# Turning the recurrent outputs of 14 tiles with VectorE and block copies instead of TensorE

## The chip, the core and the metric

The kernel runs on one core of a Trainium2 chip. The metric is the device time of one execution in microseconds; a profiled execution also gives a span, from its first to its last instruction. Engines are TensorE (PE; PEld is its weight load), VectorE (DVE), ScalarE (ACT), GpSimd (POOL) and SyncE (SP), which issues most DMAs. All arithmetic is float32 or the fp32r form of it.

## The reference

One inference step of a one-layer decoder trunk: a prompt of 2048 tokens, and 8 samples of 8 tokens. A norm and one input projection feed three groups of heads: a matrix-memory recurrence (mLSTM, 4 heads of 256), a short gated convolution, and cross-attention into 256 memory tokens. Their outputs go through one output projection, a residual add and a final norm. The change lies in the recurrence:

```python
num = (w_inter[..., None] * jnp.einsum('bthd,bhde->bhte', qb, C)
       + jnp.einsum('bhts,bshe->bhte', S, vb))
den = w_inter * jnp.einsum('bthd,bhd->bht', qb, n) + jnp.sum(S, axis=-1)
h = num / jnp.maximum(jnp.abs(den), jnp.exp(-m_t))[..., None]
C_new = w_C[..., None, None] * C + jnp.einsum('bhs,bshd,bshe->bhde', w_s, kb, vb)
...
h = jax.nn.sigmoid(heads(o_pre)) * h
h = rms_norm(h, g_head.reshape(ML_HEADS, ML_HEAD_DIM))
y_ml = h.reshape(B, T, ML_WIDTH) * jax.nn.silu(z_ml)
...
y = jnp.concatenate([y_ml, y_cv, y_xa], axis=-1) @ w_out
```

## The kernel before

The program runs in stages: the input projection with its splits (to about 1400 us), the convolution and cross-attention with their part of the output projection, and the recurrence with the rest of the output projection, from about 1605 us to the end. The change touches the last stage, the function `recur`.

There the prompt goes by in 16 tiles of 128 tokens (`NT`). Between them run 8 units for the samples: a unit has its front part in an even tile (`front_of`) and its back part in the odd tile behind (`back_of`). Each engine has one instruction stream, written out by hand in the loops over `t`; semaphores in `S` tie them together. In one tile:

- TensorE: `numerators(t)` (four heads, L2249 from the state C, L2250 from the score weights), in odd tiles the unit's numerators (L2376, L2379), then eight `update(t, j)` (L2264), one for each half head of the state, with the products of the output projection of tile t-1 between them (`out_part`, L2294 to L2296; in even tiles two parts behind each update, in odd tiles one, and eight behind the last). In odd tiles a ninth small update (L2267) and the unit's own update (L2277) follow the eighth. Then `scores(t + 1)` (L2225), the unit's front (L2360, L2362) or the turn of its output (L2387), and `turn_y(t)` (L2342): eight 128x128 transposes of the tile's output y from `th[t % 2]` into banks 3 and 4.
- The updates alternate between two banks, `DC = (0, 5)`. Update j may start when VectorE has added update j-2 to the state: `wait(pe, S["C_updated"], updates_before(t) + j - 1)`. The scores use bank 0 and wait for all updates.
- VectorE: `add(t - 2)` (L2626), `first_half(t)` (L2700 to L2709: the numerators times the output gate, the denominator), the updates of the state (L2725) with turns between them: `turn_v` (L2673), behind update 5 `final_norm(t - 2)` (L2648), behind update 6 `turn_keys(t + 1)` (L2682, from the staging tile `kb` into `kw`). Then `second_half(t)` (L2732, L2737: y times coef), in odd tiles the unit's update (L2749) and second half (L2780, L2783), `turn_o(t + 1)` (L2692), `score_weights(t + 1)` (L2618), `y_gate(t)` (L2656: y from banks 3 and 4 times z) and `y_low(t)` (L2663).
- `numerators(t)` has at its head `pe.wait_ge(S["sw_ready"], t + 1)`, the score weights of L2618.
- ScalarE: exponentials of the weights (L2450), squares for the norms (L2474, L2480), the gate's tanh (L2487), the unit's values (L2496, L2497), `keys(t + 1)` (L2458), the unit's front (L2521, L2523), `y_high(t)` (L2509).
- GpSimd: mask add (L2143) and query products (L2147) for the next tile, and small powers (L2165, L2169) for the norms, each between the squares of ScalarE and the scaling by VectorE.
- SyncE issues loads in a fixed order: in `key_squares(t)` the keys of a later tile, in 128x1024 values, into `kb`, as soon as the last ones have been turned; behind them the output gates and z.

VectorE's transpose turns each 32x32 block in its place, so a tile loaded "in squares" (`load_squares`) comes out turned as a whole.

Of the kernel before, what the change touches and what calls it, by code (L numbers as in the profile page):

```python
# [19 lines left out]
ALU = mybir.AluOpType  # L20
# [10 lines left out]
NT = T // P  # L31
# [12 lines left out]
KM = 8  # L44

SQ = 32
# [1865 lines left out]
def recur(nc, block, before, S, overlay, bank, w, ident, raw, last_y, work, wide, syhl, area, nT, mask, smask, columns, late_w, res, yh, yl,  # L1912
# [39 lines left out]
    late_h, late_l = late_w  # L1952
    LAST_X = 2 * TILES

    OUT, SPARE, DC = (6, 7), 5, (0, 5)
    SOUT, FOLD = (1, 2), (3, 4)

    def unit(u):
        return u // 4, u % 4

    def split_y(t):
# [59 lines left out]
    def _(sp):  # L2021
# [22 lines left out]
        def key_squares(t):  # L2044
            if SQUARES_FROM <= t < NT:
                wait(sp, S["keys_turned"], t - SQUARES_FROM)
                load_squares(sp, w, 2, kb[:, :], t, S["kb_loaded"])

# [83 lines left out]
    def _(pool):  # L2132
# [55 lines left out]
        pool.wait_ge(S["set"], 3)  # L2188
        for t in range(NT):
            ahead(t + 1)  # L2190
            power("squares_ready", 4 * t + 4, ssq[:, :], msq[:, :], rinv[:, :], 0.25 / HD, "rinv_ready")
            if back_of(t) is not None:
                power("s_squared", back_of(t) + 1, sssq[:, :], smsq[:, :], srinv[:, :], 0.25 / HD, "s_rinv_ready")
            if front_of(t) is not None:
                ahead_unit(front_of(t))
            if t >= 2:
                out_norm(t - 2)
        out_norm(NT - 2)
        half_norm(NT, "s_out_squared", "s_out_begun", "s_out_mean", "s_out_rstd")
# [3 lines left out]
    def _(pe):  # L2203
# [25 lines left out]
        def numerators(t):  # L2229
# [9 lines left out]
            for h in range(H):  # L2239
                if h < 2:  # L2240
                    if t < SQUARES_FROM:
                        pe.wait_ge(S["kw_ready"], 4 * t + 2 * h + 2)
                else:
                    wait(pe, S["y_gated"], 2 * (t - 1) + h - 1)
                num = bank[1 + h][:, 0:HE]
# [148 lines left out]
        for t in range(NT):  # L2394
# [34 lines left out]
            if front_of(t) is not None:  # L2429
                unit_front(t, front_of(t))  # L2430
            if t < NT - 1:
                turn_y(t)
# [11 lines left out]
    def _(act):  # L2444
# [54 lines left out]
        def y_high(t):  # L2499
# [7 lines left out]
            for i in range(2):  # L2507
                act.wait_ge(S["y_gated"], 2 * t + i + 1)
                act.activation(split_y(t)[0][:, 4 * i:4 * i + 4, :], z[:, 4 * i:4 * i + 4, :], ACT.Copy).then_inc(S["y_high"], 1)  # L2509

        def store(s):
            act.wait_ge(S["out_ready"], s + 1)
            act.dma_start(tile_rows(y_prompt[0], s), acc[s % ACC][:, :]).then_inc(S[f"y_stored{s % ACC}"], 16)
# [23 lines left out]
        for t in range(NT):  # L2537
# [12 lines left out]
            if front_of(t) is not None:  # L2550
                unit_vo_back(front_of(t))
            keys(t + 1)
            if front_of(t) is not None:
                unit_front(front_of(t))
# [31 lines left out]
    def _(dve):  # L2586
# [64 lines left out]
        def y_gate(t):  # L2651
            dve.wait_ge(S["z_loaded"], 16 * (t + 1))
            for i in range(2):
                zi = z[:, 4 * i:4 * i + 4, :]
                dve.wait_ge(S["y_turned"], 2 * t + i + 1)
                dve.tensor_tensor(zi, bank[3 + i].ap().rearrange("p (f t) -> p f t", f=4), zi,  # L2656
                                  ALU.mult).then_inc(S["y_gated"], 1)
# [26 lines left out]
        def turn_o(t):  # L2684
# [5 lines left out]
            wait(dve, S["s_squared"], units_before(t))  # L2690
            wait(dve, S["y_turned"], 2 * (t - 1))
            dve.transpose(th[t % 2], vo[:, 1, :]).then_inc(S["o_turned"], 1)  # L2692
# [34 lines left out]
        def second_half(t):  # L2727
# [7 lines left out]
            for h in range(H):  # L2735
                y = th[p][:, h * HD:(h + 1) * HD]
                dve.tensor_scalar(y, y, coef[:, h:h + 1], None, ALU.mult).then_inc(S["y_ready"], 1)  # L2737

        def n_of(u):
# [58 lines left out]
        for t in range(NT):  # L2798
# [6 lines left out]
            for j in range(8):  # L2805
                update(t, j)
                if j in (1, 3):
                    turn_v(t + 1, j // 2)
                if j == 6:
                    turn_keys(t + 1)  # L2810
                if j == 5 and t >= 2:
                    final_norm(t - 2)
                if j in (4, 5) and t == 0:
                    last_add(j - 4)
            second_half(t)
            if t == NT - 1:
# [62 lines left out]
```

## Time and profile before

| | |
|---|---|
| time, median of 3 runs | 2020.84 us (2015.42 to 2021.22) |
| profiled execution | 2021.7 us, span 2019.8 us |
| granted TensorE clock, mean | 0.999 of full speed |
| TensorE busy | 2008.2 us, 99% |
| VectorE busy | 1474.5 us, 73% |
| ScalarE busy | 912.9 us, 45% |
| GpSimd busy | 874.6 us, 43% |

Busy time of TensorE counts matmuls whose ends are modelled, and they overlap: what an instruction costs is read from the distance of the starts. The times in a timeline are microseconds from the start of the span. "issue" as releaser means a wait whose releaser the profile doesn't show.

### The profile page before, as it was taken

Reading aid. Unit: us, or ns where it says so; the run is one execution under the profiler, and the core shown is the slowest. Engines: PE = TensorE matmul, PEld = TensorE weight load, DVE = VectorE, ACT = ScalarE, POOL = GpSimd, SP = SyncE. Lnnn points to the kernel's source line nnn. Section 1 sums busy time; section 2 is a strip of 40 time slices with the busy share of each in tenths; the row PEclk is TensorE's granted clock in tenths of the full one; section 3 lists DMA queues with packets and bytes.
Section 4 is the critical chain, followed back from the end, with each engine's and each line's share of the span. In section 5 each row is a group of like instructions: output and inputs, shape, how many; then the busy total and the mean of one; then the engine's idle time right before and its main releaser. Section 6 shows DMA issues by size and latency. Waiting matters only on the chain.

```text
span 2019.8 us, 34158 instructions
## 1 busy us (share of the span) xinstructions
PE 2008.2 (99%) x12151; PEld 1877.8 (93%) x12151; DVE 1474.5 (73%) x2336; ACT 912.9 (45%) x1863; POOL 874.6 (43%) x721
## 2 busy tenths in 40 slices
PE   9999999999999999999999999999999999999998
PEld 6999999999999999999999999998888888888886
DVE  7777787798778877897778767654445468777775
ACT  5554445445444455454454455442324333433332
POOL 2556555585555565575555555520000122222220
PEclk9999999999999999999999999999999999999999
DMA  6655667555646676555445566578746788888765
GB/s 205 155 142 142 150 152 162 128 141 124 152 122 152 158 171 134 137 143 122 120 131 138 126 157 144 134 212 188 172 115 183 201 250 261 272 239 237 235 180 121
DMA packets 600151, 333.69 MB, mean 165 GB/s; under 512 B 331296, under 2 KB 563888, under 8 KB 599984
## 3 DMA queue, kind: packets, MB, share of 16 engines
q1 hardware_dynamic: 561824, 312.90, 59.5%
q10 hardware_dynamic: 37008, 14.43, 2.9%
q0 software_dynamic: 1152, 4.19, 0.6%
q8 instruction: 98, 1.61, 0.4%
q14 instruction: 69, 0.57, 0.1%
HBM read 237.87 MB, written 93.58 MB: 164 GB/s over the span
## 4 chain that ended last, share of the span: by engine, by line
PE 93%; DVE 2%; SPq 2%; DMA 1%; issue 1%; ACT 0%; POOL 0%; DVEq 0%; POOLq 0%; ACTq 0%
PE bank L742 21%; PE bank L744 21%; PE bank L743 21%; PE bank L2294 3%; PE bank L2296 2%; PE bank L2295 2%; PE bank L2264 2%; PE bank L2249 2%; PE bank L1650 1%; PE bank L1651 1%; PE bank L1652 1%; PE bank L1636 1%; PE bank L1639 1%; PE bank L1637 1%; PE bank L1601 1%; PE bank L1566 1%
## 5 line engine op out<-in xcount | busy, mean ns | idle before, releaser
L742 PE MATMUL bank<-xh,wh 128*128 128x352 f32 x2688 | 869.3, 323 | 0.9 <-DVE stage L1111 0.9
L744 PE MATMUL bank<-xh,wl 128*128 128x352 f32 x2688 | 867.0, 323 | 0.0
L743 PE MATMUL bank<-xl,wh 128*128 128x352 f32 x2688 | 863.6, 321 | 0.0
L1093 DVE TENSOR_TENSOR wl<-raw,wh 128x512 fp32r<-128x512 f32 x384 | 407.4, 1063 | 166.5 <-ACT wh L881 165.5
L742 PEld LDWEIGHTS bank<-xh,wh 128*128 128x128 f32 x2688 | 504.6, 188 | 3.8 <-issue 2.0
L743 PEld LDWEIGHTS bank<-xl,wh 128*128 128x128 f32 x2688 | 507.4, 189 | 0.3 <-issue 0.2
L744 PEld LDWEIGHTS bank<-xh,wl 128*128 128x128 f32 x2688 | 506.3, 188 | 0.0
L903 ACT ACTIVATE snap<-bank 128x352 f32<-128x352 f32 x384 | 178.5, 465 | 374.3 <-PE bank L744 374.2
L881 ACT ACTIVATE wh<-raw 128x512 fp32r<-128x512 f32 x384 | 240.6, 628 | 156.8 <-PE bank L744 155.6
L1093 DVE TENSOR_TENSOR wl<-wt,wh 128x512 fp32r<-128x512 f32 x288 | 246.8, 860 | 85.1 <-ACT wh L881 84.2
L692 POOL TENSOR_TENSOR stage<-snap 128x352 f32<-128x352 f32 x96 | 100.8, 1050 | 440.7 <-ACT snap L903 428.1
L881 ACT ACTIVATE wh<-wt 128x512 fp32r<-128x512 f32 x288 | 180.2, 626 | 118.9 <-PE bank L744 112.7
L676 POOL TENSOR_TENSOR wt<-raw 128x512 f32<-128x512 f32 x96 | 153.6, 1600 | 56.0 <-DMA raw<-in_w_in 42.1
L683 POOL TENSOR_TENSOR wt<-raw,wt 128x512 f32<-128x512 f32 x96 | 154.8, 1613 | 49.8 <-DVE wl L1093 49.8
L1111 DVE TENSOR_TENSOR stage<-bank,snap 128x352 f32<-128x352 f32 x288 | 149.0, 517 | 34.8 <-PE bank L744 30.6
L2143 POOL TENSOR_TENSOR work<-area,mask 128x512 f32<-128x512 f32 x16 | 20.7, 1295 | 336.8 <-DMA area<-scr_a 211.2
L679 POOL TENSOR_TENSOR wt<-raw,wt 128x512 f32<-128x512 f32 x96 | 156.0, 1625 | 8.1 <-DVE wl L1093 0.7
L680 POOL TENSOR_TENSOR raw<-raw 128x512 f32<-128x512 f32 x96 | 158.7, 1653 | 0.0
L2294 PE MATMUL bank<-wm_h,out_yh 128*128 128x512 f32 x240 | 117.1, 488 | 0.0
L2296 PE MATMUL bank<-wm_h,out_yl 128*128 128x512 f32 x240 | 94.3, 393 | 0.0
L2295 PE MATMUL bank<-wm_l,out_yh 128*128 128x512 f32 x240 | 94.0, 392 | 0.0
L2725 DVE SCALAR_TENSOR_TENSOR m_wide<-m_wide,wcb,bank 128x257 f32<-128x257 f32 x120 | 56.9, 475 | 49.6 <-PE bank L2264 48.4
(346 smaller groups left out, 2599.0 us busy)
## 6 DMA issues: line engine op xcount, KB each, us to landing
raw<-in_w_in SPq DMA_DIRECT2D x72, 1024.0 KB, 5.8
raw<-in_w_in SPq DMA_DIRECT2D x48, 512.0 KB, 5.6
scr_vob<-stage SPq DMA_DIRECT2D x192, 88.0 KB, 3.6
scr_qk<-stage SPq DMA_DIRECT2D x48, 352.0 KB, 5.2
raw<-scr_qk SPq DMA_DIRECT2D x16, 1024.0 KB, 8.8
area<-scr_vob SPq DMA_DIRECT2D x32, 512.0 KB, 8.0
scr_acc<-x_res SPq DMA_DIRECT2D x17, 512.0 KB, 6.2
m_acc<-scr_acc SPq DMA_DIRECT2D x17, 512.0 KB, 7.6
```

Source lines behind the costliest of these rows:

```text
L676: pool.tensor_tensor(wt[:, 0], b12, b11, ALU.subtract).then_inc(S["t_ready"], 1)
L679: pool.tensor_tensor(wt[:, 1], b22, wt[:, 0], ALU.subtract).then_inc(S["t_ready"], 1)
L680: pool.tensor_tensor(b12, b22, b12, ALU.subtract).then_inc(S["t_ready"], 1)
L683: pool.tensor_tensor(wt[:, 2], b21, wt[:, 1], ALU.subtract).then_inc(S["t_ready"], 1)
L742: pe.matmul(out, wh[:, b, k, :], xh[:, b, k, :], start=(first and k == 0), stop=False, skip_group_check=True)
L743: pe.matmul(out, wh[:, b, k, :], xl[:, b, k, :], start=False, stop=False, skip_group_check=True)
L744: m = pe.matmul(out, wl[:, b, k, :], xh[:, b, k, :], start=False, stop=(k == 3), skip_group_check=True)
L881: act.activation(halves(q, b)[0], source(q, b), ACT.Copy).then_inc(S["w_high"], 1)
L903: act.activation(snap[:, n, :], g if n == 1 else b, ACT.Copy).then_inc(S["snap"], 1)
L1093: dve.tensor_tensor(low, source(q, b), high.bitcast(F32), ALU.subtract).then_inc(S["w_low"], 1)
L1111: dve.tensor_tensor(out, src, snap[:, add, :], ALU.add).then_inc(S["out_dve"], 1)
L2294: pe.matmul(out, h[:, k, :], wmh[:, k, c], start=(k == 0), stop=False)
```

## The change

The outputs of tiles 1 to 14 (`IN_BLOCKS`) are no longer transposed by TensorE. VectorE turns `th[t % 2]` (128x1024) in 32x32 blocks into the staging tile `kb` with one instruction. The 16 blocks of partitions and columns are then carried back into `th[t % 2]` at their place, in copies of 32 partitions by 8x32 values: 8 by ScalarE, 8 by GpSimd. `y_gate` then reads `th` in SBUF instead of the banks. As the source of the turn must be ready earlier, in these tiles the key turn and the second half stand behind update 5, the turn of y behind update 6 and the final norm behind update 7. The load of the next keys into `kb` waits for both sets of copies. Tiles 0 and 15 stay as they were.

```diff
+    ysq = kb[:, :].rearrange("p (k f t) -> p k f t", f=4, t=SQ)
+    IN_BLOCKS = range(1, NT - 1)
+    BLOCKS = [(a, f) for a in range(4) for f in range(4)]
+    ACT_MOVES, POOL_MOVES = BLOCKS[:8], BLOCKS[8:]
...
+    def y_moved(t, a, f):
+        return th[t % 2].rearrange("p (k x) -> p k x", k=KM)[SQ * f:SQ * (f + 1), :, SQ * a:SQ * (a + 1)]
...
         def key_squares(t):
             if SQUARES_FROM <= t < NT:
                 wait(sp, S["keys_turned"], t - SQUARES_FROM)
+                wait(sp, S["y_moved"], len(ACT_MOVES) * (t - SQUARES_FROM))
+                wait(sp, S["y_carried"], len(POOL_MOVES) * (t - SQUARES_FROM))
                 load_squares(sp, w, 2, kb[:, :], t, S["kb_loaded"])
...
+            if t - 1 in IN_BLOCKS:
+                pool.wait_ge(S["y_carried"], len(POOL_MOVES) * (t - 1))
             ahead(t + 1)
...
             if t >= 2:
                 out_norm(t - 2)
+            if t in IN_BLOCKS:
+                pool.wait_ge(S["y_squared"], t)
+                pool.wait_ge(*((S["out_rstd"], t - 1) if t >= 2 else (S["s_rinv_ready"], back_of(t) + 1)))
+                for a, f in POOL_MOVES:
+                    pool.tensor_copy(y_moved(t, a, f), ysq[SQ * a:SQ * (a + 1), :, f, :]).then_inc(S["y_carried"], 1)
...
-                else:
-                    wait(pe, S["y_gated"], 2 * (t - 1) + h - 1)
+                elif t == 1:
+                    pe.wait_ge(S["y_gated"], h - 1)
+                elif h == 2:
+                    wait(pe, S["s_vo_ready"], sum(front_of(x) is not None for x in range(t)))
...
-            if t < NT - 1:
+            if t < NT - 1 and t not in IN_BLOCKS:
                 turn_y(t)
...
+        def y_moves(t):
+            act.wait_ge(S["y_squared"], t)
+            for a, f in ACT_MOVES:
+                act.activation(y_moved(t, a, f), ysq[SQ * a:SQ * (a + 1), :, f, :], ACT.Copy).then_inc(S["y_moved"], 1)
...
         def y_gate(t):
             dve.wait_ge(S["z_loaded"], 16 * (t + 1))
+            if t in IN_BLOCKS:
+                dve.wait_ge(S["y_moved"], len(ACT_MOVES) * t)
+                dve.wait_ge(S["y_carried"], len(POOL_MOVES) * t)
+                for i in range(2):
+                    zi, c = z[:, 4 * i:4 * i + 4, :], slice(512 * i, 512 * (i + 1))
+                    dve.tensor_tensor(zi, th[t % 2][:, c].rearrange("p (f t) -> p f t", f=4), zi,
+                                      ALU.mult).then_inc(S["y_gated"], 1)
+                return
...
+        def turn_y(t):
+            dve.wait_ge(S["y_ready"], 4 * t + 4)
+            dve.transpose(kb[:, :], th[t % 2]).then_inc(S["y_squared"], 1)
...
                 if j in (1, 3):
                     turn_v(t + 1, j // 2)
+                if t in IN_BLOCKS:
+                    if j == 5:
+                        turn_keys(t + 1)
+                        second_half(t)
+                    if j == 6:
+                        turn_y(t)
+                    if j == 7 and t >= 2:
+                        final_norm(t - 2)
+                    continue
```

TensorE at the end of an odd tile, before (`raw` holds queries and keys, `m_s_o` the unit's output, `m_wide` here y and then the scaled queries):

```order
L2296 MATMUL bank<-wm_h,out_yl 128x512
L2225 MATMUL bank<-raw 128x128 x8
L2387 MATMUL bank<-ident,m_s_o 128x128 x2
L2342 MATMUL bank<-ident,m_wide 128x128 x8
L2249 MATMUL bank<-m_wide 128x257 x2
L2250 MATMUL bank<-area,work 128x257
```

and now, with the line numbers of the changed kernel:

```order
L2317 MATMUL bank<-wm_h,out_yl 128x512
L2244 MATMUL bank<-raw 128x128 x8
L2408 MATMUL bank<-ident,m_s_o 128x128 x2
L2270 MATMUL bank<-m_wide 128x257 x2
L2271 MATMUL bank<-area,work 128x257
```

The eight transposes between the scores and the numerators are gone; nothing took their place.

VectorE in an odd tile from update 4 on, before (`m_kb` is the staging tile `kb`, the unnamed 128x257 products are the updates):

```order
L2673 STREAM_TRANSPOSE area<-area 128x2x256
L2725 SCALAR_TENSOR_TENSOR m_wide<-m_wide,wcb,bank 128x257 x2
L2648 SCALAR_TENSOR_TENSOR m_acc<-m_acc,m_few,m_gf 128x1024
L2725 SCALAR_TENSOR_TENSOR m_wide<-m_wide,wcb,bank 128x257
L2682 STREAM_TRANSPOSE m_wide<-m_kb 128x1024
L2725 SCALAR_TENSOR_TENSOR m_wide<-m_wide,wcb,bank 128x257
L2732 SCALAR_TENSOR_TENSOR m_few<-m_few 128x4
L2737 TENSOR_SCALAR m_wide<-m_wide,m_few 128x256 x4
L2716 TENSOR_TENSOR m_s_C<-m_s_C,m_wide 128x8
```

and now:

```order
L2709 STREAM_TRANSPOSE area<-area 128x2x256
L2761 SCALAR_TENSOR_TENSOR m_wide<-m_wide,wcb,bank 128x257 x2
L2718 STREAM_TRANSPOSE m_wide<-m_kb 128x1024
L2768 SCALAR_TENSOR_TENSOR m_few<-m_few 128x4
L2773 TENSOR_SCALAR m_wide<-m_wide,m_few 128x256 x4
L2761 SCALAR_TENSOR_TENSOR m_wide<-m_wide,wcb,bank 128x257
L2777 STREAM_TRANSPOSE m_kb<-m_wide 128x1024
L2761 SCALAR_TENSOR_TENSOR m_wide<-m_wide,wcb,bank 128x257
L2676 SCALAR_TENSOR_TENSOR m_acc<-m_acc,m_few,m_gf 128x1024
L2752 TENSOR_TENSOR m_s_C<-m_s_C,m_wide 128x8
```

Key turn and second half moved ahead of update 6, the turn of y was added ahead of update 7, and the final norm went behind it. The even tiles have the same order without the last row.

## Rows read from the trace of the kernel before

**Rows 1.** The chain of waits of the whole page, by engine (share of the span).

```profile
PE 93%; DVE 2%; SPq 2%; DMA 1%; issue 1%; ACT 0%; POOL 0%; DVEq 0%; POOLq 0%; ACTq 0%
```

**Rows 2.** Line L2342, output transposes: ns min/median/max, first and last start, forms.

```profile
L2342 PE MATMUL bank<-ident,area x64: 272/273/307, 1620.8 to 1968.0; 128*128 128x128 f32 x64
```

**Rows 3.** Timeline, end of an even tile (start us, length us, engine, line; idle before, releaser).

```profile
1720.64 0.69 DVE L2618 SCALAR_TENSOR_TENSOR work<-bank,work 128x512 f32<-128x512 f32 x1 [0.34 <-issue]
1720.85 0.94 PEld L2342 LDWEIGHTS bank<-ident,area 128*128 128x128 f32 x8
1721.76 0.74 PEld L2249 LDWEIGHTS bank<-m_wide 128*128 128x128 f32 x4
```

**Rows 4.** Timeline, end of an odd tile.

```profile
1746.86 0.69 DVE L2618 SCALAR_TENSOR_TENSOR work<-bank,work 128x512 f32<-128x512 f32 x1 [2.52 <-issue]
1747.62 0.73 PEld L2249 LDWEIGHTS bank<-m_wide 128*128 128x128 f32 x4
```

**Rows 5.** Timeline, tile 0 to 1, where TensorE waits for the score weights.

```profile
1621.25 0.65 DVE L2618 SCALAR_TENSOR_TENSOR work<-bank,work 128x512 f32<-128x512 f32 x1
1621.98 0.73 PEld L2249 LDWEIGHTS bank<-m_wide 128*128 128x128 f32 x4 [0.30 <-issue]
```

**Rows 6.** Timeline, updates 5 to 8 of an odd tile.

```profile
1734.98 0.48 DVE L2725 SCALAR_TENSOR_TENSOR m_wide<-m_wide,wcb,bank 128x257 f32<-128x257 f32 x1 [0.65 <-PE bank L2264]
1736.96 1.24 DVE L2682 STREAM_TRANSPOSE m_wide<-m_kb 128x1024 f32<-128x1024 f32 x1
...
1737.51 0.64 PEld L2267 LDWEIGHTS bank<-m_few,work 128*128 128x128 f32 x4
1738.12 0.44 DVE L2725 SCALAR_TENSOR_TENSOR m_wide<-m_wide,wcb,bank 128x257 f32<-128x257 f32 x1
1738.49 0.15 DVE L2732 SCALAR_TENSOR_TENSOR m_few<-m_few 128x4 f32<-128x4 f32 x1
1739.73 0.17 DVE L2716 TENSOR_TENSOR m_wide<-m_wide 128x8 f32<-128x8 f32 x1
```

**Rows 7.** Timeline, updates 5 to 7 of an even tile and the scores behind them.

```profile
1762.59 0.48 DVE L2725 SCALAR_TENSOR_TENSOR m_wide<-m_wide,wcb,bank 128x257 f32<-128x257 f32 x1 [1.32 <-PE bank L2264]
1766.66 0.48 DVE L2725 SCALAR_TENSOR_TENSOR m_wide<-m_wide,wcb,bank 128x257 f32<-128x257 f32 x1 [0.63 <-PE bank L2264]
1767.85 1.95 PE L2225 MATMUL bank<-raw 128*128 128x128 f32 x16
1769.89 0.69 DVE L2618 SCALAR_TENSOR_TENSOR work<-bank,work 128x512 f32<-128x512 f32 x1 [0.34 <-issue]
```

**Rows 8.** Timeline, tile 2.

```profile
1665.96 1.29 DVE L2648 SCALAR_TENSOR_TENSOR m_acc<-m_acc,m_few,m_gf 128x1024 f32<-128x1024 f32 x1 [2.65 <-POOL m_few L2169]
1669.22 2.05 PE L2225 MATMUL bank<-raw 128*128 128x128 f32 x16 [0.96 <-DVE m_wide L2725]
```

**Rows 9.** Timeline, VectorE's low halves: with GpSimd idle, and beside GpSimd.

```profile
1624.21 1.29 DVE L2663 TENSOR_TENSOR out_yl<-area,out_yh 128x512 fp32r<-128x512 f32 x2 [0.16 <-ACT out_yh L2509]
...
1723.21 1.82 DVE L2663 TENSOR_TENSOR out_yl<-area,out_yh 128x512 fp32r<-128x512 f32 x2 [0.16 <-ACT out_yh L2509]
```

**Rows 10.** Timeline, GpSimd's products of queries.

```profile
1609.69 2.79 POOL L2147 TENSOR_TENSOR m_wide<-raw,area 128x256 f32<-128x256 f32 x4
...
1723.42 1.07 POOL L2147 TENSOR_TENSOR m_wide<-raw,area 128x256 f32<-128x256 f32 x1 [0.65 <-PE bank L2250]
```

**Rows 11.** GpSimd's smallest one-input instruction, by form: busy us, mean ns | idle before.

```profile
L2165 POOL TENSOR_SCALAR m_few<-m_few 128x4 f32<-128x4 f32 x16 | 3.1, 193 | 66.1 <-ACT area L2474 41.8 <-ACT m_wide L2474 24.2
```

**Rows 12.** Timeline, ScalarE: four key copies of 128x256 in a row.

```profile
1766.07 1.71 ACT L2458 ACTIVATE m_kw<-m_kw,wsc 128x256 f32<-128x256 f32 x4 [0.58 <-DVE m_kw L2682]
```

**Rows 13.** Timeline, start of an odd tile: update 0 on VectorE, update 2 on TensorE.

```profile
1729.59 0.47 DVE L2725 SCALAR_TENSOR_TENSOR m_wide<-m_wide,wcb,bank 128x257 f32<-128x257 f32 x1
1730.95 0.60 PE L2264 MATMUL bank<-area,m_kw 128*128 128x257 f32 x2
```

**Rows 14.** The key staging tile: its loads, issue to landing.

```profile
DMA to landing us min/median/max: 3.6/8.4/10.6
```

More of the change, by code:

```diff
@@ L1959, in unit, with turned_by_pe @@
         return u // 4, u % 4
+    def y_moved(t, a, f):
+        return th[t % 2].rearrange("p (k x) -> p k x", k=KM)[SQ * f:SQ * (f + 1), :, SQ * a:SQ * (a + 1)]
+    def turned_by_pe(t):
+        return 2 * sum(x not in IN_BLOCKS for x in range(t))
     def split_y(t):
@@ L2552, in _ @@
             keys(t + 1)
+            if t in IN_BLOCKS:
+                y_moves(t)
             if front_of(t) is not None:
@@ L2652, in y_gate @@
             dve.wait_ge(S["z_loaded"], 16 * (t + 1))
+            if t in IN_BLOCKS:
[6 more added lines that the diff above has]
+                return
             for i in range(2):
                 zi = z[:, 4 * i:4 * i + 4, :]
-                dve.wait_ge(S["y_turned"], 2 * t + i + 1)
+                dve.wait_ge(S["y_turned"], turned_by_pe(t) + i + 1)
                 dve.tensor_tensor(zi, bank[3 + i].ap().rearrange("p (f t) -> p f t", f=4), zi,
@@ L2690, in turn_o @@
             wait(dve, S["s_squared"], units_before(t))
-            wait(dve, S["y_turned"], 2 * (t - 1))
+            wait(dve, S["y_gated"], 2 * (t - 1))
             dve.transpose(th[t % 2], vo[:, 1, :]).then_inc(S["o_turned"], 1)
@@ L2808, in _ @@
                     turn_v(t + 1, j // 2)
+                if t in IN_BLOCKS:
+                    if j == 5:
[6 more added lines that the diff above has]
+                    continue
                 if j == 6:
@@ L2814, in _ @@
                     last_add(j - 4)
-            second_half(t)
+            if t not in IN_BLOCKS:
+                second_half(t)
             if t == NT - 1:
```

## The prediction

> **What bounds the kernel now.** I read the chain of waits first: TensorE holds 93% of it [rows 1]. An edit therefore counts only through what it does to TensorE's row of work. The change touches the recurrent stage alone, about 1610 to 2019 us, so I read the timeline there: all engines around the end of an even and of an odd tile [rows 3, 4], then VectorE's updates [rows 6, 7]. The reader should look for one thing: who arrives last at each point where TensorE needs another engine. In the steady pairs of tiles TensorE never waits. The pattern repeats every 49.25 us (score weights at 1720.64 and 1769.89 [rows 3, 7]), so one pair stands for all.
>
> **What is removed.** Eight transposes a tile in 14 tiles, 112 in all. The page gives each 272 ns [rows 2], but they overlap: from the first weight load of the eight to the next instruction's load it is 1720.85 to 1721.76, 0.91 us [rows 3]. That is 14 x 0.91 = 12.7 us of TensorE, and a reader who stops here forecasts 2009.
>
> But these transposes stand in a particular gap. TensorE computes the scores of tile t+1, VectorE turns them into score weights (L2618, 0.69 us), and the numerators of t+1 wait for these weights at their head. The transposes are what TensorE did meanwhile. Tile 0 to 1 shows the wait when it decides: L2618 ends at 1621.90 and the numerators' first weight load starts at 1621.98, after 0.30 us of idleness [rows 5]; so release costs 0.08 us.
> - End of an odd tile: L2618 runs 1746.86 to 1747.55, so the numerators could start at 1747.63. They start at 1747.62 now [rows 4]. The gain is nothing: the removed 0.91 us turns into a wait of the same length. Seven tiles, 0.
> - End of an even tile: there the unit's front matmuls stand in the gap too. L2618 ends at 1721.33, release at 1721.41, and the load starts at 1721.76 now [rows 3]. At most 0.35 us a tile, 2.4 us in seven.
>
> **What is moved on VectorE.** In the 14 tiles the key turn and the second half (scaling by coef) come between updates 5 and 6, the new turn of y between 6 and 7, and the final norm behind 7. Updates used to reach TensorE promptly, and TensorE needs them: update 8 of an odd tile reuses the bank of update 6 and waits until VectorE has consumed it.
> - Odd tile: update 5 starts at 1734.98, released by TensorE. Start to start, an update takes 0.40, the key turn 1.16 (1736.96 to 1738.12), the second half 1.24 (1738.49 to 1739.73) [rows 6]. So update 6 starts at 1734.98 + 0.40 + 1.16 + 1.24 = 1737.78, ends 0.47 later at 1738.25, and is seen at 1738.33. TensorE wants to load for L2267 at 1737.51 [rows 6]. The stall is 0.82 by the loads; as a load begins while the matmul in front still runs, I take 0.7 (ends 0.6 and 0.85). Nothing gives it back: all behind it, up to the scores and L2618, hangs on TensorE. 7 x 0.7 = +4.9 us.
> - Even tile: there is no update 8. Update 5 starts at 1762.59; update 6 at +2.80 = 1765.39; the turn of y at 1765.79; update 7 at 1766.95, ends 1767.43, against 1766.66 now. The scores wait for it and start at 1767.85 [rows 7]; that holds, by little. Then final norm (1.2) and gate turn (1.2) end at 1769.8, just before L2618 at 1769.89 [rows 7]. So the 0.35 of the even tile survives if nothing lengthens this chain.
>
> **What lengthens it.** GpSimd's eight copies run just beside the final norm, which reads two operands in SBUF. The nearest pair of rows: the low halves (two SBUF operands) take 1.29 us with GpSimd idle and 1.82 beside its products [rows 9]; GpSimd's product takes 0.70 alone (2.79 for four) and 1.07 beside them [rows 10]. So the final norm may cost up to 0.5 us more, and L2618 then starts at 1770.3: the even gain is anything from 0.35 down to -0.1. I take 0.2, 7 x 0.2 = -1.4 us. The gate multiply, which read PSUM and now reads two SBUF operands beside GpSimd's mask add, can lose another 0.5. The Trainium skill ("SBUF — State Buffer", who interferes with whom) says that a VectorE instruction with two SBUF inputs contends with a GpSimd instruction that reads SBUF, and this trace agrees: 1.82 against 1.29.
>
> **The copies.** ScalarE's eight, by its four key copies of 256 columns in 1.71 us [rows 12], are 8 x 0.40 = 3.3 us (ends: 0.3 to 0.5 each, for 32 partitions with strided blocks). They start when y is turned, 1767.1 in an even tile, and the unit's key scaling behind them moves to about 1770.5, 0.2 late. GpSimd's copy is not in the trace. Below it lies its smallest one-input instruction, 0.19 [rows 11]; above it the two-input product of as many columns, 0.70 alone, 1.07 contended [rows 10]. With one operand instead of two I halve what grows: 0.19 + 0.25 = 0.45, eight in 3.6 us, about 4 with contention. "GPSIMD Engine Reference" in the Trainium skill (elementwise cycle accounting) has about one cycle per element for one input and 2.6 for two; by it the copy would be near 0.4 us and the sum would not change; no row here has such a copy.
>
> When are they needed? In an odd tile y is turned at 1739.4 and gated only after L2618, 1747.6: over 8 us, ample. In an even tile y is turned at 1767.1 and the gate comes right behind L2618 and two small instructions, 1771.1: 4 us. The gate, the low halves, the add and the first half all stand ahead of the next tile's update 0, which ends at 1730.06, while TensorE's update 2, which needs its bank, starts at 1730.95, its load some 0.2 before [rows 13]. That leaves 0.6 us, or 0.25 where TensorE has become 0.35 earlier. With 4 us for the copies and up to 0.5 on the gate, I charge 0.2 in each of six or seven odd tiles: +1.2 us.
>
> **Loads.** The next keys are now loaded into the staging tile only after the copies: in an even tile about 1771.2, in an odd one 1743.5. They land 8.4 us later, 10.6 at most [rows 14], by 1782 and 1754; they are wanted by 1784.6 (49.25 behind 1735.4) and 1763. Hidden; if the cover went, each us late is a us on updates 6. The output gates' load queued behind it slips 2 us into ScalarE slack.
>
> **Tile 2** has a hiccup: VectorE waits 2.65 us for a norm ahead of update 6, and TensorE's scores wait 0.96 for update 7 [rows 8]. The new order puts that norm behind update 7, so these 0.96 us go: -1.0.
>
> **Sum.** +4.9 - 1.4 + 1.2 - 1.0 = +3.7 us. The profiled execution took 2021.7 us (span 2019.8), so it would be 2025.4; the median before is 0.9 lower, hence 2024.5.
>
> **Rivals.**
> - A, the removed work comes back as time: 12.7 us less, near 2009. For it: TensorE is 93% of the chain. Against it: rows 4. It would need TensorE's numerators to be released by something other than L2618, or VectorE's updates not to be awaited at update 8. The milder form (no stall at update 8, even gain 0.35 whole, tile 2) is -3.4, about 2017.4. This is the other side; it decides if update 6 ends before 1737.4 in an odd tile.
> - B, the GpSimd copies end last. If one costs 0.70, eight take 5.6, 1.2 us beyond the room of about 4.4, in seven tiles +8.4; at 1.07, 8.6 us, 4.2 late, +29. With the stall at update 8 that is 2033 to 2053. For it: SBUF contention in rows 9 and 10; against it: one input only.
> - C, the contention is worse than its rows (final norm and turn both held, updates of even tiles later than 1767.5, so that the scores wait as well): another 0.3 to 0.5 in each of 14 tiles, 2029 to 2032.
>
> **Chances.** Forecast 0.55 (its own range 2021 to 2028); A 0.18, of it two thirds the mild form; B 0.15; C 0.12. About 0.3%, 6.1 us, is what can be told from no change: the borders are 2014.8 and 2026.9. Faster is strong A: 0.06. Slower is B, C and the upper fifth of the forecast: 0.37. The rest, 0.57, is no change. The range for 8 in 10 reaches from the mild A to the lower end of B: 2017 to 2036.
>
> **What would show it.** Right: L2342's successor shows only 16 transposes of y; a wait on L2618 at the head of the numerators, 0.8 to 0.9 us in odd tiles and 0.3 to 0.5 in even ones; a wait of TensorE for update 6 at update 8, near 0.7, seven times. The even gate multiply is released by L2618's chain, not by GpSimd. Wrong: no wait at update 8 (then A), a GpSimd copy over 0.55 us (then B), scores waiting for update 7 in even tiles (then C), key turns waiting for their load.

## The result: 0.8% slower, and the profile after

| | before | changed |
|---|---|---|
| time, median of 6 runs each | 2021.03 us (2015.42 to 2024.06) | 2037.64 us (2035.27 to 2041.93) |
| profiled execution, span | 2019.8 us | 2034.1 us |
| TensorE busy | 2008.2 us | 2002.9 us |
| GpSimd busy | 874.6 us | 943.6 us |

The ratio is 1.0082, 95% interval 1.007 to 1.0094. The forecast was 2024.5 us with a range to 2036: the sign of its sum was right, its size wrong by 13 us, and the measured time lies outside the range.

The page of the changed kernel, busy times and the chain of waits by engine:

```profile
PE 2002.9 (98%) x12039; PEld 1865.4 (92%) x12039; DVE 1507.0 (74%) x2350; ACT 959.4 (47%) x1975; POOL 943.6 (46%) x833
...
PE 90%; DVE 6%; issue 1%; POOL 1%; SPq 0%; ACT 0%; DMA 0%; DVEq 0%; POOLq 0%; ACTq 0%
```

The chain has moved from TensorE to VectorE, 2% before [rows 1] and 6% now. So TensorE waits. Where, the view of the waits of TensorE in the recurrent stage tells (engine, tile, line, what it waited for: us in total, times, longest):

```profile
PE bank L2285 <- DVE m_s_o L2806: 10.7, 6, 1.9
PE bank L2270 <- issue: 6.9, 14, 0.7
PE bank L2288 <- DVE m_wide L2761: 2.7, 7, 0.4
```

The second and the third were forecast: the head of the numerators and update 8. The first, the largest, was not. It is at update 1 of the odd tiles. The timeline of the changed kernel from the end of an even tile (12, score weights at 1721.69) to update 1 of the next, odd one; it answers to [rows 3, 13]:

```profile
1718.86 4.48 POOL L2216 COPY area<-m_kb 32x256 f32<-32x256 f32 x8 [6.48 <-DVE m_kb L2777]
...
1719.09 1.27 DVE L2676 SCALAR_TENSOR_TENSOR m_acc<-m_acc,m_few,m_gf 128x1024 f32<-128x1024 f32 x1
...
1721.69 0.69 DVE L2646 SCALAR_TENSOR_TENSOR work<-bank,work 128x512 f32<-128x512 f32 x1 [0.18 <-issue]
...
1722.45 0.73 PEld L2270 LDWEIGHTS bank<-m_wide 128*128 128x128 f32 x4 [0.39 <-issue]
...
1723.06 0.19 DVE L2799 SCALAR_TENSOR_TENSOR m_wide<-bank,m_wide 128x32 f32<-128x32 f32 x1 [0.60 <-ACT work L2549]
...
1723.42 1.27 POOL L2155 TENSOR_TENSOR work<-area,mask 128x512 f32<-128x512 f32 x1
...
1723.47 2.90 DVE L2686 TENSOR_TENSOR area<-area 128x512 f32<-128x512 f32 x2 [0.22 <-POOL area L2216]
...
1724.65 4.59 POOL L2159 TENSOR_TENSOR m_wide<-raw,area 128x256 f32<-128x256 f32 x4
...
1726.29 2.35 DVE L2699 TENSOR_TENSOR out_yl<-area,out_yh 128x512 fp32r<-128x512 f32 x2
...
1728.56 1.27 DVE L2654 TENSOR_TENSOR m_acc<-m_acc,bank 128x512 f32<-128x512 f32 x2
...
1729.28 0.70 PE L2285 MATMUL bank<-area,m_kw 128*128 128x257 f32 x2
...
1731.87 0.41 DVE L2806 SCALAR_TENSOR_TENSOR m_s_o<-m_s_o,bank 128x256 f32<-128x256 f32 x1
...
1732.53 0.67 PE L2285 MATMUL bank<-area,m_kw 128*128 128x257 f32 x2 [1.87 <-DVE m_s_o L2806]
```

Three things are to be seen. The numerators start 0.76 behind the start of the score weights, as predicted. The gate multiply (L2686) starts 1.78 behind them and its pair takes 2.90, the low halves (L2699) 2.35. And TensorE, after update 0 at 1729.28, sits until VectorE has finished L2806 for update 1. The same place of the kernel before, in its timeline:

```profile
1721.78 1.28 DVE L2656 TENSOR_TENSOR area<-bank,area 128x512 f32<-128x512 f32 x2
...
1724.96 1.27 DVE L2626 TENSOR_TENSOR m_acc<-m_acc,bank 128x512 f32<-128x512 f32 x2
...
1728.59 0.70 PE L2264 MATMUL bank<-area,m_kw 128*128 128x257 f32 x2
...
1728.80 0.41 DVE L2766 SCALAR_TENSOR_TENSOR m_s_o<-m_s_o,bank 128x256 f32<-128x256 f32 x1
...
1729.58 0.42 PEld L2264 LDWEIGHTS bank<-area,m_kw 128*128 128x128 f32 x2
...
1729.81 0.60 PE L2264 MATMUL bank<-area,m_kw 128*128 128x257 f32 x2
```

There the gate's pair took 1.28, and L2766 (L2806 now) ended at 1729.21. Update 1 started its matmuls 0.60 behind that end, at 1729.81. In the changed kernel, where it waits for this end (1732.28), it starts 0.25 behind it, at 1732.53. So the room was 0.35 us.

The end of the odd tile, from update 6 to the next numerators, answers to [rows 4, 6]:

```profile
1740.55 0.48 DVE L2761 SCALAR_TENSOR_TENSOR m_wide<-m_wide,wcb,bank 128x257 f32<-128x257 f32 x1
...
1741.08 0.61 PE L2288 MATMUL bank<-m_few,work 128*128 128x4 f32 x4 [0.39 <-DVE m_wide L2761]
...
1742.24 4.49 POOL L2216 COPY m_wide<-m_kb 32x256 f32<-32x256 f32 x8 [4.38 <-DVE m_kb L2777]
1742.46 1.27 DVE L2676 SCALAR_TENSOR_TENSOR m_acc<-m_acc,m_few,m_gf 128x1024 f32<-128x1024 f32 x1
...
1750.31 0.69 DVE L2646 SCALAR_TENSOR_TENSOR work<-bank,work 128x512 f32<-128x512 f32 x1 [1.85 <-issue]
...
1751.11 1.11 PE L2270 MATMUL bank<-m_wide 128*128 128x257 f32 x4 [0.68 <-issue]
1751.12 2.36 DVE L2686 TENSOR_TENSOR area<-m_wide,area 128x512 f32<-128x512 f32 x2
1751.18 1.75 POOL L2155 TENSOR_TENSOR work<-area,mask 128x512 f32<-128x512 f32 x1 [4.45 <-DVE work L2646]
```

Update 8 (L2288) waits for update 6, and the removed transposes have become a wait of 0.68 at the numerators.

**Where the time went.** I measured TensorE from start to start in every tile. One steady pair took 49.25 us and takes 51.66:

| TensorE, start to start, us | before | changed | difference |
|---|---|---|---|
| even tile, scores to numerators | 3.28 | 2.84 | -0.44 |
| odd tile, numerators to update 0 | 6.72 | 6.80 | +0.08 |
| odd tile, update 0 to 1 | 1.22 | 3.25 | +2.03 |
| odd tile, update 1 to 2 | 1.14 | 1.20 | +0.06 |
| odd tile, update 7 to 8 and what restarts behind it | 1.13 | 1.67 + 0.1 | +0.66 |
| odd tile, scores to numerators, and on to update 0 | 2.87 + 5.25 | 2.84 + 5.28 | 0 |

From tile 0's scores to tile 15's, 15.0 us were added: tiles 5, 7, 9 and 11 2.4 each, tile 13 4.0, tile 3 1.75, tiles 0 and 1 0.8 together, tile 2 gave back 1.15 [rows 8]; the span grew by 14.3.

**Tile 15 shows what the wait at update 1 needs.** It is the last tile, and at the end of tile 14 GpSimd has no mask add and no products left to do. The gate starts as late there as elsewhere, 1.78 behind the score weights (1981.61):

```profile
1983.39 1.29 DVE L2686 TENSOR_TENSOR area<-area 128x512 f32<-128x512 f32 x2 [0.22 <-POOL area L2216]
...
1984.84 1.29 DVE L2699 TENSOR_TENSOR out_yl<-area,out_yh 128x512 fp32r<-128x512 f32 x2 [0.16 <-ACT out_yh L2530]
...
1990.42 0.60 PE L2285 MATMUL bank<-area,m_kw 128*128 128x257 f32 x2
```

Both pairs take 1.29, L2806 ends 8.21 behind the score weights instead of 10.59, and update 1 follows update 0 by 1.22 without a wait. So the late start of the gate and its new source cost no time by themselves. The wait comes only with GpSimd's mask add and products beside VectorE's pairs.

Tile 13 is longer than its neighbours by 1.6, and its waits don't tell why. The windows of TensorE do (window, its length, busy us and instructions, granted clock, DMA share, GB/s):

```profile
1936.00:1940.00 4.00, 2.15 (x9) 1.00 0.92 241
1940.00:1944.00 4.00, 4.00 (x12) 0.57 0.41 34
1941.00:1942.00 1.00, 1.00 (x4) 0.50 0.49 29
```

TensorE was busy 2.15 of 4 us while it waited for update 1, and then the granted clock was 0.57 in the mean of 4 us and 0.50 inside them, 1.2 GHz instead of 2.4. A wait here can cost more than its length. That the wait brought the clock down is read from their order in time; no run shows it by itself.

### The profile page after: what moved, and what is told of

Read it like the earlier page. It is cut to its first block, busy times and chain, and to the rows that moved or that the text cites. A ratio compares the mean times of both kernels' runs of the same rounds, so it can differ in the third digit from the quotient of the medians.

```text
span 2034.1 us, 34185 instructions
## 1 busy us (share of the span) xinstructions
PE 2002.9 (98%) x12039; PEld 1865.4 (92%) x12039; DVE 1507.0 (74%) x2350; ACT 959.4 (47%) x1975; POOL 943.6 (46%) x833
## 4 chain that ended last, share of the span: by engine, by line
PE 90%; DVE 6%; issue 1%; POOL 1%; SPq 0%; ACT 0%; DMA 0%; DVEq 0%; POOLq 0%; ACTq 0%
PE bank L742 21%; PE bank L744 21%; PE bank L743 21%; PE bank L2315 2%; PE bank L2317 2%; PE bank L2316 2%; PE bank L2285 2%; PE bank L2270 2%; PE bank L1650 1%; PE bank L1651 1%; PE bank L1652 1%; PE bank L1636 1%; PE bank L1637 1%; PE bank L1639 1%; PE bank L1601 1%
```

## The experiments

The times of all are set against the kernel before on the same chip. "Gap" is TensorE's distance from update 0 to update 1 in a steady odd tile: 1.22 before, 3.25 after the change. The executions of the kernel before spread from 2015.4 to 2024.1, so a mechanism is read from the profiled executions, and the medians say only whether the time moved.

**e1, VectorE's order alone**, on the kernel before; the transposes stay on TensorE.

```diff
                 if j in (1, 3):
                     turn_v(t + 1, j // 2)
+                if 1 <= t < NT - 1:
+                    if j == 5:
+                        turn_keys(t + 1)
+                        second_half(t)
+                    if j == 7 and t >= 2:
+                        final_norm(t - 2)
+                    continue
```

> Only VectorE's new order, on the kernel before: TensorE still transposes y, no copies, gate reads PSUM. Theory (three waits of TensorE: update 8 about 0.67 us, head of the next numerators 0.9 us in odd tiles, start of the odd tiles 2.1 us, the last from contention with GpSimd at the gate): only the wait at update 8 is here, 7 x 0.67 = +4.7 us, less about 1.0 us of tile 2, so +3.7 us against before (2021), and no wait of TensorE at update 1. Rival (the order alone makes VectorE late everywhere): a wait at update 1 here too, +10 us or more.

Measured 2025.97 us (2024.54 to 2028.94), ratio 1.0039 (1.0025 to 1.0053); the medians are 7.0 us apart and the profiled spans 4.3, where 3.7 was expected. TensorE's waits in its trace:

```profile
PE bank L2267 <- DVE m_wide L2725: 2.7, 7, 0.4
```

The distance to update 8 is 1.67 in seven odd tiles, update 1 waits nowhere, and tile 2 lost its hiccup (24.19 to 23.04). Tile 1 alone became 1.1 us longer. The term for update 8 stands as predicted, and it is due to the order, not to the copies.

**e2, the gate reads SBUF**, on the kernel before. TensorE still transposes y, but in tiles 1 to 14 the gate leaves the result aside and multiplies the y that isn't turned. A wait that keeps this y until the gate has read it is not shown in the cut.

```diff
+                dve.wait_ge(S["y_ready"], 4 * t + 4)
+                src = th[t % 2][:, 512 * i:512 * (i + 1)] if 1 <= t < NT - 1 else bank[3 + i].ap()
-                dve.tensor_tensor(zi, bank[3 + i].ap().rearrange(...), zi, ALU.mult)
+                dve.tensor_tensor(zi, src.rearrange(...), zi, ALU.mult)
```

> Only the gate's source, on the kernel before: in tiles 1 to 14 the gate multiply reads y in SBUF instead of the banks. It leaves out the full transpose of y (what it reads is not turned); TensorE still does its transposes. Theory (the gate with two SBUF operands is held up beside GpSimd's mask add and query products): the gate's pair takes 2.4 to 2.9 us instead of 1.28, the low halves no less than 1.8, and TensorE waits 1.0 to 1.5 us at update 1 of the seven odd tiles: +7 to +11 us. Rival (the copies end late, the source costs nothing): pair at 1.3 us, no wait, same time as before.

Measured 2022.21 us (2017.44 to 2023.53), ratio 1.0011 (1.0 to 1.0021). From its timeline at the same place:

```profile
1720.73 2.14 DVE L2658 TENSOR_TENSOR area<-area 128x512 f32<-128x512 f32 x2
...
1722.37 1.10 POOL L2147 TENSOR_TENSOR m_wide<-raw,area 128x256 f32<-128x256 f32 x1 [0.65 <-PE bank L2250]
...
1723.03 2.12 DVE L2665 TENSOR_TENSOR out_yl<-area,out_yh 128x512 fp32r<-128x512 f32 x2 [0.16 <-ACT out_yh L2509]
```

A miss. The mechanism shows (gate pair 2.14 against 1.28, low halves 2.12 against 1.82, gap 1.50), and the 0.63 by which VectorE's chain grew less the room of 0.35 is the growth of the gap. But at 0.35 us for each odd tile it is a sixth of the effect. GpSimd's products still wait for TensorE between each other here, and VectorE gets through in their pauses; the mask add is 0.28 ahead of the gate. In the changed kernel it starts with the gate, and the products run back to back.

**e3, GpSimd's mask add and products behind the gate**, on the changed kernel.

```diff
                 pool.wait_ge(S["y_carried"], len(POOL_MOVES) * (t - 1))
+                pool.wait_ge(S["y_gated"], 2 * t)
```

> The changed kernel, with GpSimd's mask add and query products held until the gate multiply is done. Theory (contention at the gate): the gate's pair falls to about 1.3 us, the wait at update 1 of odd tiles from 2.0 to about 0.6, seven times, so 8 to 10 us less than the changed kernel, about 2028. Rival (the late copies decide): at most 1 us less. Rival (waits of ScalarE for the masks come in its place): no gain, ScalarE waiting for GpSimd before its squares.

Measured 2029.45 us (2026.92 to 2031.58), ratio 1.0053 (1.0036 to 1.007). Its timeline:

```profile
1721.18 1.29 DVE L2687 TENSOR_TENSOR area<-area 128x512 f32<-128x512 f32 x2 [0.22 <-POOL area L2217]
...
1722.61 1.27 POOL L2155 TENSOR_TENSOR work<-area,mask 128x512 f32<-128x512 f32 x1 [1.56 <-issue]
1722.63 2.93 DVE L2700 TENSOR_TENSOR out_yl<-area,out_yh 128x512 fp32r<-128x512 f32 x2 [0.15 <-ACT out_yh L2531]
```

The gate's pair is back at 1.29 us, and the low halves pay instead: 2.93. The contention moved on by one pair of instructions, and the gap fell only to 2.49, a wait of up to 1.2 us where 0.6 was expected.

**e4, update 6 ahead of the second half in odd tiles**, on the changed kernel.

```diff
                     if j == 5:
                         turn_keys(t + 1)
+                    if j == 5 + t % 2:
                         second_half(t)
```

> The changed kernel, with update 6 ahead of the second half in odd tiles (key turn, update 6, second half, turn of y). Theory: the wait at update 8 (L2288 of the changed kernel, 0.67 us in seven tiles) goes and nothing takes its place, -4.7 us against the changed kernel, about 2033. Rival (update 6 was not what it waited for): no change.

Measured 2030.92 us (2029.54 to 2034.05), ratio 1.0061 (1.0041 to 1.0081). The distance to update 8 is 1.13 again, and the gap at update 1 stays, 3.27. The two waits are independent, and the second half can be moved at no cost.

**e5, no GpSimd copies**, on the changed kernel. Eight of the sixteen blocks of y are not carried back, and the gate reads the y that isn't turned in their place. The three waits for these copies are gone as well; the cut leaves them out.

```diff
-                for a, f in POOL_MOVES:
-                    pool.tensor_copy(y_moved(t, a, f), ysq[SQ * a:SQ * (a + 1), :, f, :]).then_inc(S["y_carried"], 1)
```

> The changed kernel without GpSimd's eight copies (half of y's blocks stay where they were and the gate reads them so: the output of the prompt is wrong in them). Rival B of the prediction (the copies on GpSimd end last): the gate starts up to 1.5 us earlier and most of the 2.0 us wait at update 1 goes. Theory (the start of an odd tile is lost in three parts: gate released 0.64 late, gate 1.4 longer, low halves 0.5 longer): ScalarE's copies still hold the gate back, and mask add and query products fall apart again, so the gate's pair takes about 2.1 as where only its source was changed; gap between updates 0 and 1 from 3.25 to about 2.2 us, 7 to 8 us less in all.

Measured 2027.35 us (2026.49 to 2032.14), ratio 1.0037 (1.0024 to 1.005). At the same place of its trace, an even tile's end:

```profile
1726.25 0.69 DVE L2641 SCALAR_TENSOR_TENSOR work<-bank,work 128x512 f32<-128x512 f32 x1 [0.18 <-issue]
...
1727.11 1.27 POOL L2154 TENSOR_TENSOR work<-area,mask 128x512 f32<-128x512 f32 x1 [10.16 <-DVE work L2641]
...
1727.74 2.33 DVE L2680 TENSOR_TENSOR area<-area 128x512 f32<-128x512 f32 x2
...
1728.67 0.85 POOL L2158 TENSOR_TENSOR m_wide<-raw,area 128x256 f32<-128x256 f32 x1 [0.28 <-PE bank L2266]
...
1729.99 1.86 DVE L2693 TENSOR_TENSOR out_yl<-area,out_yh 128x512 fp32r<-128x512 f32 x2
```

GpSimd's mask add starts 0.86 behind the score weights instead of 1.73, its products are spread out again (1728.67 and on), the gate starts at +1.49 instead of +1.78, and the pairs take 2.33 and 1.86. The gap is 1.90: of the 2.03 us that the change added there, 1.35 hang on GpSimd's copies. By tile 15 it is not their late end that costs this, but the mask add and the products that they push back onto VectorE's pairs.

**e6, the last product of the output projection behind the next scores, in odd tiles**, on the changed kernel: it fills the wait at the numerators (the added lines stand behind the scores of t + 1).

```diff
-                for g in range(12 if t == NT - 1 else 8, 16):
+                for g in range(12 if t == NT - 1 else 8, 15 if t in IN_BLOCKS and t % 2 else 16):
                     out_part(t - 1, g)
...
+            if t in IN_BLOCKS and t % 2:
+                out_part(t - 1, 15)
```

> The changed kernel with the last part of the output projection moved behind the next scores in the odd tiles 1 to 13, into the gap where the transposes stood. Theory (there TensorE waits for the score weights as long as the removed transposes took): the scores start 0.68 us earlier and the wait at the head of the numerators goes, so an odd tile's end gets 0.8 us shorter, 7 tiles, -5 to -6 us against the changed kernel, about 2032. Rival (something else holds the numerators): wait stays, no change.

Measured 2031.31 us (2028.25 to 2035.91), ratio 1.0054 (1.0037 to 1.0071). The odd tile is 27.95 instead of 28.62, and the wait at its end is gone. That is the 0.68 us that the removed transposes had left there, and it shows that they had only been filler.

**e7, e4's order, the filler in even tiles too, and there the final norm behind the score weights** (`if t % 2 == 0: final_norm(t - 2)` behind `score_weights(t + 1)`).

> The changed kernel with update 6 ahead of the second half in odd tiles, the last part of the projection behind the next scores in tiles 1 to 14, and in even tiles the final norm behind the score weights. Theory: -0.66 (update 8) and -0.8 (head of the numerators) in each of seven odd tiles, and up to -0.4 in even ones, against the changed kernel -10 to -13 us, about 2026; the wait at update 1 stays at 2 us. Rival (VectorE becomes the bound of the whole pair): the wait at update 1 grows by what is saved elsewhere, and less than half arrives.

Measured 2029.81 us (2029.75 to 2030.08), ratio 1.0045 (1.003 to 1.006). The waits at update 8 and at the odd tile's end are gone, which is most of the gain; 10 to 13 us less than the changed kernel were expected, and by the two ratios it is 7.5. The even tile shrank from 23.04 to 22.61 only on paper: the filler now stands behind the scores, and from the scores to the numerators it is 3.17 instead of 2.84. The final norm now stands between the score weights and the gate. The gate starts 2.28 behind the score weights instead of 1.78, L2809 (L2806 of the changed kernel) ends 11.09 behind them instead of 10.59, and the gap at update 1 grew from 3.25 to 3.52. Moving the norm there lengthened the very chain for which TensorE waits, and e8 and e9 keep that edit.

**e10, the second low half behind update 1 of the next tile**, alone on the changed kernel: the VectorE chain in front of L2806 is shorter by one instruction.

```diff
+            y_low(t, (0,) if t in IN_BLOCKS else (0, 1))
...
                 update(t, j)
+                if j == 1 and t - 1 in IN_BLOCKS:
+                    y_low(t - 1, (1,))
```

> The changed kernel, with only the second low half of tiles 1 to 14 moved behind update 1 of the next tile. Theory (at update 1 of an odd tile TensorE waits for the unit's first half, and VectorE's time from the score weights to there goes straight into it): that half is 1.1 us, so the gap between updates 0 and 1 falls from 3.25 to about 2.1 us in seven tiles, -7 to -8 us against the changed kernel, about 2029.5, with 1.67 us ahead of update 8 as before. Rival (another wait right behind): no gain.

Measured 2027.66 us (2026.18 to 2028.12), ratio 1.0037 (1.0024 to 1.0049). The waits of TensorE:

```profile
PE bank L2285 <- DVE m_s_o L2806: 3.7, 5, 0.7
```

The gap fell from 3.25 to 2.11 and the wait for L2806 from 10.7 to 3.7 us, while update 8 waits as before (2.7 us in seven times). One low half taken out of the chain, 1.2 us long, shortens the gap by 1.14. That settles the path: it runs over VectorE, from the score weights by gate and low halves to L2806.

**e8, e7 and e10 together.**

> As e7_filled, and the second low half of tiles 1 to 14 behind update 1 of the next tile. Theory: VectorE reaches update 1's operands 1.1 us earlier in odd tiles, so 7 x 1.1 = 7.7 us less than e7_filled, about 2018, a little under the kernel before (2020). Rival (the next low half is then wanted by the projection, or the z load slips): no gain.

Measured 2020.7 us (2019.6 to 2024.65), ratio 1.0002 (0.9992 to 1.0011): level with the kernel before, 2.7 us above what was expected. Gap 2.39.

**e9, e8 with e3's line.**

> As e8_filled_late, and GpSimd's mask add and query products held until the gate multiply is done. Theory: at the start of odd tiles the gate's pair falls from 2.5 or 2.9 to 1.29 us and the first low half stays contended, so the gap between updates 0 and 1 falls from 2.39 to about 1.4 us, seven times: -6 to -7 us against e8_filled_late, about 2013 to 2015, the first version under the kernel before. Rival (GpSimd's products run without gaps then and hold up the low half and what follows): -2 us or less.

Measured 2016.1 us (2011.72 to 2020.48, 12 runs), ratio 0.998 (0.9971 to 0.9988). This is the first version below both kernels, by 0.2% the one before; the interval is just clear of no difference. 2013 to 2015 us and a gap of 1.4 were expected. From its timeline:

```profile
1716.05 1.29 DVE L2690 TENSOR_TENSOR area<-area 128x512 f32<-128x512 f32 x2
...
1717.48 1.27 POOL L2155 TENSOR_TENSOR work<-area,mask 128x512 f32<-128x512 f32 x1 [1.56 <-DVE area L2690]
...
1717.50 1.80 DVE L2703 TENSOR_TENSOR out_yl<-area,out_yh 128x512 fp32r<-128x512 f32 x1 [0.16 <-ACT out_yh L2534]
...
1723.19 0.67 PE L2286 MATMUL bank<-area,m_kw 128*128 128x257 f32 x2 [0.21 <-DVE m_s_o L2810]
...
1724.30 0.68 DVE L2703 TENSOR_TENSOR out_yl<-area,out_yh 128x512 fp32r<-128x512 f32 x1
```

Gate pair 1.29, one low half beside the mask add 1.80, the other undisturbed behind update 1, 0.68; the wait at update 1 is 0.21 and the gap 1.60. A pair of tiles takes 48.7 us against 49.25 before. Of the 1.8 us that the transposes cost in a pair, 0.55 has become time. None of e9's other edits was run on the kernel before; that they alone gain nothing there is argued from its steady pairs, in which TensorE never waits.

## Why the prediction was wrong

**The step that failed** is the last one of the part on the copies: "TensorE's update 2, which needs its bank, starts at 1730.95 ... I charge 0.2 in each of six or seven odd tiles: +1.2 us." Measured: 2.09 in each of five odd tiles and 1.56 in tile 3, 12.0 us in the profiled execution. The other steps missed by 1.2 us or less each, the clock aside. Three things were wrong in it:

- The consumer. It named update 2 as the first in TensorE's row that waits for VectorE's first half. In the code it is update 1 of an odd tile: `if j == 1` it waits for `s_t1_ready` and `s_den_copied` (the unit's output and denominator, L2806 and L2805), because it writes the bank in which the unit's denominator stood. The kernel printed above has these two waits; I had followed the bank of the state's updates and not the unit's. The room was not 0.6 but 0.35 us.
- The even tile's gain. It was counted as -1.4 us. It came whole, 0.35 a tile and 2.6 us in all, but it makes TensorE earlier at a place where VectorE is awaited. From the start of the score weights to update 0 it was 7.95 us and is 7.59, so TensorE is 0.36 earlier. VectorE's chain became longer by 2.02 (below), and 0.35 was room: 2.02 + 0.36 - 0.35 = 2.03, the growth of the gap from 1.22 to 3.25. The other 0.06 follow at update 2. So the gain was given back some 8 us later.
- The sizes. VectorE from the start of the score weights to the end of L2806 took 8.57 us (1720.64 to 1729.21) and takes 10.59 (1721.69 to 1732.28).

| that chain | before | changed | difference | named in the forecast |
|---|---|---|---|---|
| score weights to gate | 1.14 | 1.78 | +0.64 | 0 |
| gate to low halves | 1.43 | 2.82 | +1.39 | up to 0.5 |
| low halves to add | 1.75 | 2.27 | +0.52 | 0 |
| add to the end of L2806, with VectorE's waits, which vanish | 4.25 | 3.72 | -0.53 | |

The 0.64 has two causes: L2799, the unit's small multiply ahead of the gate, waited 0.60 for ScalarE's L2549, which stood behind the eight copies of ScalarE; and the gate then waited 0.22 for GpSimd's last copy. The forecast had ScalarE's copies right (3.49 us, 3.3 forecast) and saw the unit's key scaling move behind them, but not L2549 behind that, for which VectorE waits. For GpSimd it asked when the copies end, and not what they push: the mask add starts 1.73 behind the score weights instead of 0.86 (as in e5), hence with the gate, and the products behind it, late against TensorE, no longer pause for it. Tile 15, where they are absent, shows that this is what turns the late gate into a wait.

The copies end so late because one of the eight is held up. In tile 1, which has no final norm, each takes 0.40; where the norm runs beside them, the second takes 1.31:

```profile
L2216 POOL COPY m_wide<-m_kb x8: 387/396/400, 1639.5 to 1642.6; 32x256 f32<-32x256 f32 x8
...
L2216 POOL COPY area<-m_kb x1: 1307/1307/1307, 1719.3 to 1719.3; 32x256 f32<-32x256 f32 x1
```

It starts 0.2 behind the norm and ends 0.25 behind the norm's end. So the contention that the forecast looked for came, and GpSimd paid for it, not VectorE: 0.91 us in each of 13 tiles, and eight copies in 4.48 us instead of 3.57. Without it the copies would end 0.74 behind the score weights, ahead of the gate, and the mask add could start where it does in e5. This is an estimate; no run kept the norm away from the copies in an even tile.

**What held.** Update 8: forecast 0.7, measured 0.66 in seven odd tiles [rows 6], shown by e1 and e4. The odd tile's end: 0.9 of work became 0.68 of wait and nothing was gained [rows 4], shown by e6. Tile 2: forecast -1.0, measured -1.15 [rows 8]. The loads of the keys are never awaited. Even tiles: update 7 did not hold the scores. The final norm, which "may cost up to 0.5 us more" beside GpSimd's copies, took 1.27 as before, since it was the copy that was held up, so the even gain was 0.35 and not 0.2. The estimate of 0.45 for one copy was right; the "about 4 with contention" for eight was short by 0.5.

**The rivals.** A is out. B, "the GpSimd copies end last", is right in part, and its sign came, a copy over 0.55: one of eight takes 1.31, not each 0.70. Eight take 4.48 against a room of 4.4, so the gate waits for them, but for 0.22 only. By B's own working that costs 1.5 us; the 1.35 per tile that e5 gives them comes mostly by the work that they push. C, "the contention is worse than its rows", named the right kind of cause at the wrong place: scores wait nowhere.

**The clock** adds what no step had: 1.6 us in tile 13. In the profiled executions with the largest gap it fell once or twice in the recurrent stage ahead of its last matmuls (changed kernel, e4 and e6 once each, e7 twice, gaps of 3.25 to 3.52 us); in the kernel before, e1, e2, e3, e5, e8, e9 and e10, with gaps up to 2.57, never. So it goes together with the long gap; why one or two of five such waits bring it and the others do not stays open. In the six runs of the changed kernel the mean clock goes with the time: 0.999 at 2035.3 and 2035.9, 0.998 at 2036.9 to 2038.7, 0.997 at 2041.9.

With the failed term at 12.0 the sum would be 3.7 + 10.8 + 1.6 for the clock, 16.1, where 14.3 was measured in the span. The rest is in small terms: the even ends gave 1.2 more than charged, update 8 took 0.35 less, tile 2 gave 0.15 more, the end of tile 0 gave 0.25, the stretch ahead of the first scores was 0.35 shorter, and tile 0 was 0.4 longer. Why tile 0 was longer in this execution, where e4's was not, stays open.

## What to carry to other kernels

When work moves off the busiest engine, list every semaphore that this engine waits for in the stretch behind it, in the order of its own instructions, and measure the room of each: the first one short of room takes back the gain, and where it was earned does not matter. Count what an added instruction pushes back on its own engine as well as when it ends itself, and look at each instruction of a row of equal ones: a mean of 0.56 us hid seven copies of 0.40 and one of 1.31. Work removed from a gap that another engine sets is only a hole, until other work of the same engine is moved into it.

## What the runs showed of the hardware

**VectorE and GpSimd with two SBUF operands each nearly take turns.** The single instructions of the changed kernel at the place above, by line (duration ns min/median/max, first and last start):

```profile
L2686 DVE TENSOR_TENSOR area<-area x2: 1212/1489/1766, 1723.5 to 1725.2; 128x512 f32<-128x512 f32 x2
```

and

```profile
L2159 POOL TENSOR_TENSOR m_wide<-raw,area x4: 1173/1176/1184, 1724.6 to 1728.1; 128x256 f32<-128x256 f32 x4
```

The first gate multiply takes 1.77 beside the mask add of 1.27 and the second 1.21 beside the products; alone it takes 0.69 (e3). The products, 0.70 alone [rows 10], take 1.18. The one that starts later pays. At the end of the even tile the mask add starts 0.05 ahead of the gate and keeps its 1.27, and the gate's first multiply takes 1.77; at the end of the odd tile (1751.12 and 1751.18 above) the gate starts 0.06 ahead, and the mask add takes 1.75. The later one does not lose the whole rest of the first: 1.22 to the mask add's end and 0.69 would be 1.91, 0.14 more than the 1.77. A multiply and a product together advance one step each in about 1.14 us, where strict turns would give 0.69 + 0.70 = 1.39. My estimate from the 1.77: some 0.14 us of each instruction lies outside the turns, and 1.39 less twice 0.14 is 1.11, near the 1.14. "SBUF — State Buffer" in the Trainium skill (who interferes with whom, and the summary of rules for kernel authors) calls it an exclusive lock on a shared port, in which the second to issue blocks until the first finishes. The trace agrees on who pays and, but for that 0.14, on how much. A pair of such instructions, 1.29 alone [rows 9], costs 0.5 to 0.8 more beside products with pauses, 1.1 beside unbroken ones, and 0.9 to 1.6 when the mask add falls in with it.

**GpSimd's one-input copies contend too, and there GpSimd is the one that waits.** Beside VectorE's final norm, which reads two operands in SBUF, the norm keeps its 1.27, and the copy that starts behind it takes 1.31 instead of 0.40, in 13 of 14 tiles. In e7, where the norm of the even tiles stands later, it is the last of the eight copies that takes 1.47, and the others take 0.40. The same page of the Trainium skill (who interferes with whom) says that a VectorE instruction with two SBUF inputs contends with a GpSimd instruction that reads SBUF, and that the order of issue decides who blocks. Both hold here, for copies of 32 partitions as well.

**The price of a small GpSimd copy** of 32x256, undisturbed: 0.40 busy and 0.45 start to start (3.57 for eight, tile 1). ScalarE does the same copy in 0.42 and 0.44 start to start (3.49 for eight).
